# Moving half of a wide pair's second-half columns from TensorE to VectorE in a hybrid decoder block

## The reference, cut to what matters

```python
def peer(xn, wq, keys, u_tab, v_tab):
    def chunk(xc):                       # 128 tokens
        q = (xc @ wq).reshape(PEER_CHUNK, PEER_HEADS, PEER_DK)
        ...                              # key scores, top 16 of each half, top 16 of the pairs
        g = jax.nn.softmax(best, axis=-1)
        u = u_tab[idx]
        act = jax.nn.gelu(jnp.einsum('td,thkd->thk', xc, u))
        w = g.astype(xc.dtype) * act
        return jnp.einsum('thk,thkd->td', w, v_tab[idx])
```

## Time and profile before

| | |
|---|---|
| median of 3 runs | 3270.11 us (3268.71 to 3271.2) |
| the profiled execution, its own time | 3273.27 us |
| its span | 3271.5 us |
| PE (TensorE matmul) busy | 2409.2 us, 74% |
| DVE (VectorE) busy | 2489.9 us, 76% |
| ACT (ScalarE) busy | 1060.2 us, 32% |
| POOL (GpSimd) busy | 1568.7 us, 48% |
| bytes moved by DMA, mean rate | 1212.83 MB, 371 GB/s |
| chain that ended last | DVE 32%, PE 25%, DMA 22%, ACT 13%, issue 6% |

### The profile page before, as it was taken

One profiled execution on the slowest core, in us unless ns is written; L12 is line 12 of the kernel. 1 busy time (PEld: TensorE's weight loads), 2 busy tenths in 40 slices (PEclk: granted clock), 3 DMA queues, 4 the chain that ended last, 5 costly groups with the idle time before them and its releaser, 6 DMA issues.

```text
span 3271.5 us, 29405 instructions
## 1 busy us (share of the span) xinstructions
PE 2409.2 (74%) x7376; PEld 1267.0 (39%) x7376; DVE 2489.9 (76%) x5592; ACT 1060.2 (32%) x2377; POOL 1568.7 (48%) x1552
## 2 busy tenths in 40 slices
PE   8669887659888778676887887867678755555554
PEld 7537454236544344222554443434333311111111
DVE  1666679857778779987767888869977778887887
ACT  2232521331566511234214766522122221112111
POOL 0133333434444433454544545544555567776775
PEclk9879888879989889798888999979888977777777
DMA  6879689879978989899999999999999999999998
GB/s 232 334 286 369 226 356 375 322 274 400 382 286 316 352 355 367 341 384 390 395 418 408 377 372 419 388 420 420 384 394 419 418 401 422 422 422 400 422 422 341
DMA packets 185039, 1212.83 MB, mean 371 GB/s; under 512 B 20672, under 2 KB 20672, under 8 KB 53440
## 3 DMA queue, kind: packets, MB, share of 16 engines
q0 software_dynamic: 147456, 1073.81, 81.9%
q1 hardware_dynamic: 37440, 137.40, 10.9%
HBM read 1198.54 MB, written 12.58 MB: 370 GB/s over the span
## 4 chain that ended last, share of the span: by engine, by line
DVE 32%; PE 25%; DMA 22%; ACT 13%; issue 6%; POOL 1%; SPq 0%; DVEq 0%; POOLq 0%; ACTq 0%
DMA ring<-in_uv,cur_idx 20%; DVE ring L1115 14%; PE vacc L940 7%; PE bank L978 7%; DVE acc L1135 7%; ACT L736 4%; PE bank L1046 3%; ACT g_ge L757 2%; PE bank L974 2%; PE bank L1057 1%; ACT diag L761 1%; DVE g_w L1124 1%; PE o_ps L944 1%; DMA xn<-in_final_norm_g 1%; DVE lt L1252 1%
## 5 line engine op out<-in xcount | busy, mean ns | idle before, releaser
L940 PE MATMUL vacc<-ring,diag 128*128 128x512 f32 x1884 | 1201.0, 760 | 817.3 <-ACT diag L761 816.4
L718 POOL DMA_INDIRECT ring<-in_uv,cur_idx x1024 | 1192.7, 1165 | 1137.4 <-PE vacc L940 529.3
L1115 DVE CUSTOM_DVE_ANT_0 ring<-ring,xn 128x1024 f32<-128x1024 f32 x1024 | 1229.9, 1220 | 183.9 <-DMA ring<-in_uv,cur_idx 182.1
L940 PEld LDWEIGHTS vacc<-ring,diag 128*128 128x128 f32 x1884 | 393.6, 228 | 1458.3 <-ACT diag L761 1067.8
L1135 DVE SCALAR_TENSOR_TENSOR acc<-ring,g_w,acc 128x512 f32<-128x512 f32 x838 | 673.7, 804 | 40.5 <-DVE g_w L1124 0.3
L757 ACT ACTIVATE g_ge<-dots 128x2 f32<-128x2 f32 x512 | 104.0, 203 | 1731.4 <-DVE dots L1115 1730.3
L709 POOL COPY cur_idx<-idx 128x2 uint32<-128x2 uint32 (+1 forms) x512 | 374.1, 731 | 538.5 <-DVE acc L1135 401.6
L761 ACT ACTIVATE diag<-ident,g_w 128x128 f32<-128x128 f32 x942 | 330.7, 394 | 130.6 <-DVE g_w L1124 130.6
L978 PE MATMUL bank<-hT,wpool 128*128 128x256 f32 (+2 forms) x1280 | 291.8, 386 | 1.4 <-ACT hT L788 1.4
L1124 DVE TENSOR_TENSOR g_w<-g_ge,gate 128x2 f32<-128x2 f32 x512 | 81.9, 160 | 273.0 <-ACT g_ge L757 272.8
L736 ACT ACT_TABLE_LOAD x221 | 283.5, 1283 | 4.7 <-PEq L1400 0.8
(11 more groups left out here) (129 smaller groups left out, 1602.5 us busy)
## 6 DMA issues: line engine op xcount, KB each, us to landing
wpool<-in_w_in SPq DMA_DIRECT2D x96, 512.0 KB, 7.6
wpool<-in_peer_wq SPq DMA_DIRECT2D x64, 512.0 KB, 8.4
wpool<-in_w_out SPq DMA_DIRECT2D x32, 512.0 KB, 7.8
ring<-in_uv,cur_idx POOLq DMA_INDIRECT x1024, 10.2
xb<-in_x SPq DMA_DIRECT2D x15, 512.0 KB, 8.0
x_scratch<-xb SPq DMA_DIRECT2D x8, 512.0 KB, 8.2
xn_scratch<-xb SPq DMA_DIRECT2D x8, 512.0 KB, 11.4
xn<-xn_scratch SPq DMA_DIRECT2D x8, 512.0 KB, 8.4
```

The lines of the kernel that those rows point to most:

```text
L718: nc.gpsimd.indirect_dma_start(ring[:, s, :], None, uv, bass.IndirectOffsetOnAxis(ap=cur_idx[:, s:s + 1], axis=0))\
L940: ins = nc.tensor.matmul(vacc[:, :], diag[:, q, s, :], ring[:, q * GROUP + s, D:D + PE_COLS], start=first and s == 0, stop=last and s == G ...
L1115: ins = nc.vector.tensor_tensor_reduce(out=ring[:, s, 0:D], in0=ring[:, s, 0:D], in1=xn[:, c % 2, :], scale=1.0, scalar=0.0, op0=ALU.mult, ...
```

## The change

In a wide pair, the matmul into `o_ps` (line 944) is issued for slot 1 only. For slot 0, VectorE adds the second 512 columns, by the same `add_rows` that ordinary pairs use. A new constant `DVE_SLOTS_WIDE = 1` says how many slots that is. `add_rows` gets the number of slots that VectorE takes, and its last add raises `s_vd` for all that are left, so in a wide pair one add raises it by 2. The matmuls into `vacc`, the diagonals, the order of the work and all other pairs stay as they were.

```diff
+DVE_SLOTS_WIDE = 1
...
-                    if wide:
+                    if wide and s >= DVE_SLOTS_WIDE:
                         ins = nc.tensor.matmul(o_ps[:, :], diag[:, q, s, :], ring[:, q * GROUP + s, D + PE_COLS:2 * D],
-                                               start=first_wide and s == 0, stop=last and s == GROUP - 1,
+                                               start=first_wide and s == DVE_SLOTS_WIDE, stop=last and s == GROUP - 1,
                                                skip_group_check=True)
...
                     weights(c, i, q, G, sl)
-                    if is_wide(c, i, q):
-                        dve.sem_inc(s_vd, GROUP)
-                    else:
-                        add_rows(c, G, q, first, pe_slots(c, i, q))
+                    add_rows(c, G, q, first, pe_slots(c, i, q), DVE_SLOTS_WIDE if is_wide(c, i, q) else GROUP)
                     return
...
-            def add_rows(c, G, q, first, by_pe):
+            def add_rows(c, G, q, first, by_pe, by_dve):
                 dve.wait_ge(s_gw, G + 1)
-                for k in range(GROUP):
+                for k in range(by_dve):
...
-                                                   op0=ALU.mult, op1=ALU.add).then_inc(s_vd, 1)
+                                                   op0=ALU.mult, op1=ALU.add).then_inc(s_vd, 1 if k + 1 < by_dve else GROUP - k)
```

## The result

The changed kernel takes 3295.19 us (median of 6 runs, 3290.9 to 3301.72) against 3269.86 us for the one before in the same comparison (3264.18 to 3272.7). The ratio is 1.0076, with a 95% interval of 1.0066 to 1.0087: slower by 25 us (22 to 28). The forecast was 3299 us, slower by 29.

The account below looks back on a forecast made before the run. VectorE was taken to bound the wide pairs of chunks 0 and 2, gathers those of chunk 5. 7.0 + 22.4 - 3 + 3 = +29.4 us on the median 3270.11 gave 3299 us, range 3285 to 3326.

Parts of the forecast that it names:

- Which engine sets the pace: Wide pairs of chunks 0 and 2 run at VectorE's pace, those of chunk 5 at the gathers' pace.
- The price of an add: In each of the 93 wide pairs, one 512-column add costs VectorE 0.79 us, 73.5 us in all.
- Stretch A: Chunk 0's 15 wide pairs, 561 to 661 us: 14 adds count, less shorter waits, +7.0 us.
- The shorter wait before `look_up`: Chunk 0's wide pairs: adds lie in three waits for ScalarE's copies before `look_up`, -2.4 us.
- Stretch B: Chunk 2's 33 wide pairs, 1353 to 1530 us: 32 adds count, less shorter waits, +22.4 us.
- the waits for gelu: Chunk 0's wide pairs: these waits stand before the add, which can't shorten them, 0 us.
- Given back after A and B: After chunk 0's and 2's wide pairs, the gathers' lead shortens later waits: -3 us, bounds 0 and -6.4.
- Stretch C: Chunk 5's 45 wide pairs, 2388 to 2611 us: nearly all adds fall into VectorE's waits, +3 us, bounds 0 and +34.8.
- that C saturates: Rival, chunk 5's wide pairs: VectorE falls behind, all adds count, 3331 us; chance 0.14, wholly or in good part.
- that TensorE's release sets the gathers' pace: Rival, chiefly chunk 5: TensorE sets when gathers start, so the change is faster, 3253 us; chance 0.05.
- That TensorE's fallen clock makes C longer: Smaller saturation variant, chunk 5's wide pairs: less busy TensorE clocks lower, +8 us; a quarter of 0.14 lies between.
- That later waits take up the whole loss: Rival: later waits for gathers absorb the adds of chunks 0 and 2, nothing to be seen, 3270 us; chance 0.05.

Follow-up runs that it names:

- the doubled load: VectorE adds the second 512 columns of both slots in chunk 5's wide pairs, chunks 0 and 2 as in the kernel before: 3292.75 us, ratio 1.0063.
- the relief alone: Against the kernel before, TensorE drops slot 0's second half in all 93 wide pairs and nobody adds it: 3268.86 us, ratio 0.9988.

## Why the prediction was right

The direction, the mechanism and the place were right: A and B pay, C doesn't. By its own steps:

- **Which engine sets the pace.** Right in all three stretches, and the list of VectorE's waits told it. The test of it is the doubled load: C pays once the adds exceed the waits for gathers.
- **The price of an add.** 0.79 us taken, 0.79 measured over B (0.76 where a dot follows, 0.80 where a search step does).
- **Stretch A**: +7.0 predicted, +6.4 measured (+6.5 with the change in chunk 0 alone). The shorter wait before `look_up` was worth 7.4 - 4.8 = 2.6 us, predicted 2.4. For the end, where the last add and the missing matmul both shorten VectorE's wait, I had 0.8 + 1.7 = 2.5; the wait went from 6.2 to 3.5, 2.7.
- **Stretch B**: +22.4 predicted, +19.6 measured, 2.8 us less. The end gave 2.1 us (4.6 to 2.5) where I had 0.5 + 0.8 = 1.3. And the waits for gelu, which I had said the add can't shorten, fell from 14.4 to 12.8. Nearly all of that is in two pairs of `look_up`, whose waits of 2.58 and 2.49 us became 1.79 each, an add's length less: there an add of the pair ahead does give ScalarE time. A new wait of 0.4 us stands against it. With the 0.8 at the end that makes 2 of the 2.8 us; the rest is within the scatter.
- **Given back after A and B**: -3 predicted, 0 measured. From the final sum of chunk 0 to that of chunk 1 it is 453.3 us before and 453.1 after; from chunk 2's to chunk 3's 377.0 and 377.7. This is the term that failed. By these lengths alone it isn't settled, because over kernels with the same code there they scatter by 3 to 4 us (452.4 to 456.4 and 374.1 to 377.8). The waits say more: in the 360 us behind A VectorE waits 18.1 us for gathers where it was 15.5, and in 121 us behind B 20.7 where it was 19.8. With chunk 0 alone it is 11.8 behind A, but 11.2 to 15.5 in kernels that leave A alone, so no shortening shows. The lead itself came about: from the issue of a gather to the dot that uses it, the average over 26 gathers near the end of B (the 101st to 126th of chunk 2) is 12.95 us before and 16.25 after, 3.3 us more, as worked out. But it lay idle. In the 30 us behind B VectorE has no wait for gathers at all, in either kernel; these are all of its waits in the changed one, 1556 to 1587:

```profile
DVE g_w L1122 <- ACT g_ge L758: 7.3, 5, 5.1
DVE acc L1371 <- PE o_ps L945: 2.5, 1, 2.5
DVE acc L1379 <- DMA xn<-in_final_norm_g: 0.8, 1, 0.8
```

and in the kernel before, 1560 to 1590, the waits for gathers begin, 4.0 us (after, 1587 to 1617: 3.8):

```profile
DVE ring L1115 <- DMA ring<-in_uv,cur_idx: 4.0, 4, 1.9
```

By then the ring has gone round once at VectorE's pace, and the places have been issued anew, as late as VectorE freed them. Gather by gather, the time from issue to dot is longer than before by 2.8, 1.2, 1.9 and 0.8 us for the first four of chunk 3, and from the 7th to the 22nd it is the same to within 0.2 us, but for one. So the lead was gone before the first wait that it could have shortened. This is read from the two traces; no run took it apart by itself.
- **Stretch C**: +3 predicted, -0.6 measured. VectorE's reserve of a few per cent was enough, and the +3 put on it was not needed. The index copies did get longer beside the adds, as weighed: in C they wait 10.8 us for the add and take 567 ns each (479 before), and the gathers keep their 410 GB/s:

```profile
L710 POOL COPY cur_idx<-idx 128x2 uint32<-128x2 uint32 x45 | 25.5, 567 | 11.0 <-DVE acc L1133 10.8
```

In B the average went from 642 ns to 704, a sixth of the way to the 1021 of ordinary pairs; I had said half.

With 7.0 + 22.4 + 3 too high by 7 us and -3 too low by 3, the errors partly made up for each other: 29.4 against 25.4. That much of the forecast's closeness is luck.

Of the rivals, that C saturates fell with the change in chunk 5 alone, and that TensorE's release sets the gathers' pace fell with the relief alone. That TensorE's fallen clock makes C longer fell too: the clock fell from 0.88 to 0.82 there, and C did not grow. That later waits take up the whole loss fell with chunks 0 and 2 alone (7.5 and 15.7 us); that they take up a small part of it is spoken against by the traces only.

TensorE's busy share was no guide here. Where VectorE never waits for gathers, or the gathers are at their full rate, a freed TensorE was worth 4 us in all (1 to 7).

## What to carry to other kernels

Before work is moved from one engine to another, list what the receiving engine waits for in each stretch: the waits for something that comes no sooner are the room it has, and that room (42.7 us in C, none for gathers in A and B) told the price of the same instruction to within 4 us a stretch. The lead that a buffer gives was of use here only up to one round of the buffer, and no wait came within it. And when a move costs in one direction, try the opposite one in the smallest step: one matmul a pair brought 9.5 us where two lost 9.8.

## What the runs showed of the hardware that was not expected

TensorE's granted clock followed its load down: with three matmuls a pair instead of four the mean fell from 0.92 to 0.80 in B, and with two, in the doubled load of chunk 5, to 0.69 (2385 to 2629 us; 0.88 before in the earlier trace rows):

```profile
2385.00:2629.00 244.00, 141.77 (x180) 45.76 (x180) 220.87 (x501) 59.25 (x155) 132.31 (x134) 0.69 0.97 381
```

What TensorE did between: in C its idle time in front of the `vacc` matmuls, waiting for the diagonals, grew from 45 to 72 to 104 us, and the records got longer (before; changed; doubled load):

```profile
L940 PE MATMUL vacc<-ring,diag 128*128 128x512 f32 x183 | 108.5, 679 | 45.5 <-ACT diag L761 45.4
L941 PE MATMUL vacc<-ring,diag 128*128 128x512 f32 x184 | 114.5, 754 | 72.0 <-ACT diag L762 72.0
L944 PE MATMUL vacc<-ring,diag 128*128 128x512 f32 x183 | 144.5, 936 | 103.8 <-ACT diag L765 103.8
```

So the work taken off TensorE shortened its busy time by less than its own length, because what was left ran slower. Over the whole kernel the mean of an `o_ps` record rose from 660 ns to 717.
